# A two-layer decoder trunk on one core: compressed keys normed earlier, memory values split in halves, a lagging values product, gathers moved into the expert block

## The reference

```python
# layer 0 (even): sparse attention (8 heads, 2 kv groups) beside gated linear attention
q = rope(rmsnorm(q, q_g), positions)
kc = rope(rmsnorm(compress(k_cmp), k_g[0]), pos_blk_end)    # 31 compressed blocks
p_c = masked_softmax(einsum('bsghd,bcgd->bghsc', q, kc) * scale, mask_c)
o_c = einsum('bghsc,bcgd->bsghd', p_c, vc)
# selected-block branch o_s and sliding-window branch o_w, each softmax(q k) v
o = g0 * o_c + g1 * o_s + g2 * o_w
# every layer: cross-attention into mem (256 positions, 4 heads of 256)
kv = rmsnorm(mem, mem_g) @ wkv;  k = rmsnorm(kv[:, :, 0]);  v = kv[:, :, 1]
# every layer: 16 experts, top 2 of one group of 4
y = sum over e of gates[:, e] * ((silu(gu[:, :384]) * gu[:, 384:]) @ w_out[e]),  gu = t @ w_in[e]
```

## Time and profile before

| | before |
|---|---|
| median of 3 runs | 1619.91 us (1617.14 to 1620.81) |
| profiled execution | 1616.9 us, span 1614.8 |
| TensorE busy | 1451.3 us, 90% |
| VectorE busy | 977.9 us, 61% |
| ScalarE busy | 770.5 us, 48% |
| GpSimd busy | 142.8 us, 9% |
| mean granted TensorE clock | 0.951 |
| last projection ends | 160.4 us |
| compressed block, attention block | 168.5 to 192.9, to 310.9 us |
| expert blocks begin | 652.6 and 1357.7 us |

### The profile page before, as it was taken

One profiled execution on the slowest core, in us unless ns is written; L12 is line 12 of the kernel. 1 busy time (PEld: TensorE's weight loads), 2 busy tenths in 40 slices (PEclk: granted clock), 3 DMA queues, 4 the chain that ended last, 5 costly groups with the idle time before them and its releaser, 6 DMA issues. The chain is left out here.

```text
span 1614.8 us, 19652 instructions
## 1 busy us (share of the span) xinstructions
PE 1451.3 (90%) x7753; PEld 1221.7 (76%) x7753; DVE 977.9 (61%) x1297; ACT 770.5 (48%) x1124; POOL 142.8 (9%) x159
## 2 busy tenths in 40 slices
PE   6999698879899888799999599999999896999993
PEld 5788566667688666799997478887887585999982
DVE  4473657574646436699996522455244526999974
ACT  3412555374424424577774233432143524877761
POOL 1000011200000000222211000000000002222210
PEclk9999799879999999899999799999999997999997
DMA  6723121032252043799986532321522064899965
GB/s 195 138 57 107 36 72 53 1 105 95 74 213 79 27 151 144 258 381 374 376 340 238 189 105 81 102 79 53 186 67 77 1 243 185 338 368 387 373 257 207
DMA packets 111005, 274.96 MB, mean 170 GB/s; under 512 B 41777, under 2 KB 44226, under 8 KB 106306
## 3 DMA queue, kind: packets, MB, share of 16 engines
q1 hardware_dynamic: 95506, 203.96, 36.5%
q10 hardware_dynamic: 5904, 52.96, 8.3%
q0 software_dynamic: 9504, 16.80, 2.8%
HBM read 266.27 MB, written 25.17 MB: 180 GB/s over the span
## 5 line engine op out<-in xcount | busy, mean ns | idle before, releaser
L185 DVE TENSOR_TENSOR w_lo<-w_stage,w_hi 128x2048 fp32r<-128x2048 f32 (+2 forms) x32 | 67.2, 2104 | 187.3 <-ACT w_hi L175 177.4
L175 ACT ACTIVATE w_hi<-w_stage 128x2048 fp32r<-128x2048 f32 (+2 forms) x36 | 63.9, 1780 | 235.0 <-PE bank L240 154.9
L200 DVE TENSOR_TENSOR w_lo<-w_stage,w_hi 128x2048 fp32r<-128x2048 f32 x42 | 96.1, 2289 | 62.0 <-ACT w_hi L194 36.1
L194 ACT ACTIVATE w_hi<-w_stage 128x2048 fp32r<-128x2048 f32 x38 | 72.7, 1915 | 101.6 <-PE bank L240 65.3
L2871 PE MATMUL bank<-e_wi_lo,e_hx_hi 128*128 128x384 f32 x256 | 86.7, 339 | 0.0
L2870 PE MATMUL bank<-e_wi_lo,e_hx_hi 128*128 128x384 f32 x256 | 86.6, 338 | 0.0
L240 PE MATMUL bank<-w_hi,h_sg_hi 128*128 128x512 f32 x192 | 76.6, 399 | 4.1 <-DVE h_sg_lo L2293 2.1
L2726 DVE TENSOR_TENSOR e_wi_lo<-e_room,w_hi 128x1536 fp32r<-128x1536 f32 x40 | 68.6, 1752 | 11.6 <-ACT w_hi L2722 11.4
L240 PE MATMUL bank<-w_hi,h_sg_lo 128*128 128x512 f32 x192 | 75.3, 392 | 0.0
L240 PE MATMUL bank<-w_lo,h_sg_hi 128*128 128x512 f32 x192 | 75.3, 392 | 0.0
L2730 POOL DMA_INDIRECT e_tok<-moe_h,moe_slots x32 | 64.7, 2021 | 114.3 <-DVE moe_slots L2430 78.5
(11 more groups left out here) (529 smaller groups left out, 4194.2 us busy)
## 6 DMA issues: line engine op xcount, KB each, us to landing
e_room<-in_moe_w_in SPq DMA_DIRECT2D x88, 768.0 KB, 10.5
w_stage<-in_moe_w_in SPq DMA_DIRECT2D x40, 768.0 KB, 8.3
e_wo<-in_moe_w_out ACTq DMA_DIRECT2D x16, 1536.0 KB, 10.7
e_room<-in_moe_w_out ACTq DMA_DIRECT2D x14, 1536.0 KB, 11.1
w_stage<-in_x_wkv SPq DMA_DIRECT2D x16, 1024.0 KB, 5.3
w_stage<-in_sg_w_in SPq DMA_DIRECT2D x16, 1024.0 KB, 5.2
w_stage<-in_hyb_w_in SPq DMA_DIRECT2D x10, 1024.0 KB, 5.1
w_stage<-in_x_wq SPq DMA_DIRECT2D x8, 1024.0 KB, 5.1
```

Source lines behind the costliest of these rows:

```text
L175: act.activation(self.w_hi[h][:, :, :cols], self.stage[h][:, :, :cols], ACT.Copy)\
L185: dve.tensor_tensor(self.w_lo[h][:, :, :cols], self.stage[h][:, :, :cols], self.w_hi[h][:, :, :cols], ALU.subtract).then_inc(self.lo_done[ ...
L194: act.activation(self.w_hi[h][:, :, :cols], self.stage[h][:, :, :cols], ACT.Copy).then_inc(self.hi_done[h], 1)
L200: engine.tensor_tensor(self.w_lo[h][:, :, :cols], self.stage[h][:, :, :cols], self.w_hi[h][:, :, :cols], ALU.subtract).then_inc(self.lo_do ...
```

## The change

Four edits. First, in `hybrid_front` the root and the rest of the key norm move ahead of `group(LAST)`, and with them w_hi and w_lo of the first half of the memory value weights. Second, in `compressed_branch` TensorE makes the products of that half for both memory tiles (`values_half(pe, 0)`, 24 matmuls) after the scores; they go to banks 5 and 7, so scores use banks 2 and 3 and the transposes 6 and 4. VectorE adds the gates after the softmax's subtraction, and the w_lo half that stood ahead of the mask add is gone. Third, in `nsa_attention` the other half (`values_half(pe, 1)`) stands ahead of unit 0, units 1 and 2 lose their pieces, the eight pieces of group 3 move to units 3 to 6 and 8 to 11, its splits from units 3 and 4 to units 1 and 2, probT has two buffers, and TensorE issues the weighted product of unit u - 1 after the scores (and piece) of unit u. Fourth, the gathers of experts 0 and 1 and two w_lo quarters move from the end of `moe_front` to the start of `moe_experts`, in both layers.

```diff
@@ -612,9 +612,10 @@
                     act.activation(act1[:, kv, 0:N_CMP], m.psum[5 + kv][:, 0:N_CMP], ACT.Gelu_apprx_tanh).then_inc(gelued, 1)
                 act.wait_ge(out2, 2)
                 act.activation(vc[0:N_CMP], m.psum[7][0:N_CMP, P:2 * P], ACT.Copy).then_inc(v_here, 1)
-                group(LAST)
                 act.wait_ge(kc_mean, 1)
                 act.activation(kc_sq[0:N_CMP, 0, 0:KVH], kc_ss[0:N_CMP], ACT.Sqrt).then_inc(kc_root, 1)
+                m.half_hi(act, mkv.first, 0)
+                group(LAST)
...
@@ -714,12 +715,13 @@
                 link(dve.tensor_tensor(kc_sq[0:N_CMP], kc[0:N_CMP], kc[0:N_CMP], ALU.mult))
                 link(dve.tensor_reduce(kc_ss[0:N_CMP], kc_sq[0:N_CMP], AX.X, ALU.add))
                 dve.tensor_scalar(kc_ss[0:N_CMP], kc_ss[0:N_CMP], 1.0 / HD, EPS, ALU.mult, ALU.add).then_inc(kc_mean, 1)
-                group(LAST)
                 dve.wait_ge(kc_root, 1)
                 link(dve.reciprocal(kc_ss[0:N_CMP], kc_sq[0:N_CMP, 0, 0:KVH]))
                 link(dve.tensor_tensor(kc_n[0:N_CMP], kc[0:N_CMP], kc_ss[0:N_CMP].unsqueeze(2).to_broadcast([N_CMP, KVH, HD]), ALU.mult))
                 link(dve.tensor_tensor(kc_n[0:N_CMP], kc_n[0:N_CMP], kc_gain[0:N_CMP].unsqueeze(1).to_broadcast([N_CMP, KVH, HD]), ALU.mult))
                 rotate(dve, link, kc_r[0:N_CMP], kc_n[0:N_CMP], cos[0:N_CMP, T], sin[0:N_CMP, T], kc_tmp[0:N_CMP], KVH).then_inc(kc_done, 1)
+                m.half_lo(dve, mkv.first, 0)
+                group(LAST)
...
@@ -780,14 +782,15 @@
                     for h in range(HPG):
                         for g in range(KVH):
                             c0 = (i * HPG + h) * CP
-                            ins = pe.matmul(m.psum[4 + g][:, c0:c0 + CP], qkT[g * HD:(g + 1) * HD, h, i * P:(i + 1) * P],
+                            ins = pe.matmul(m.psum[2 + g][:, c0:c0 + CP], qkT[g * HD:(g + 1) * HD, h, i * P:(i + 1) * P],
                                             kcT[g * HD:(g + 1) * HD, :], start=True, stop=True)
                             if i == T - 1 and h == HPG - 1:
                                 ins.then_inc(scored[g], 1)
+                kv.values_half(pe, 0)
                 pe.wait_ge(normed, 1)
                 for g in range(KVH):
                     for i in range(T):
-                        ins = pe.transpose(m.psum[6 + g][:, i * P:(i + 1) * P],
+                        ins = pe.transpose(m.psum[6 - 2 * g][:, i * P:(i + 1) * P],
...
@@ -800,7 +803,7 @@
             @block.scalar
             def _(act):
                 kv.split_first_hi(act)
-                m.split_hi(act, kv.first)
+                m.half_hi(act, kv.first, 1)
...
-                dve.wait_ge(gb_in, 16)
-                dve.wait_ge(ga_t, 1)
-                dve.tensor_tensor(ga[:, :, :], m.psum[0][:, 0:T * 3 * HEADS].rearrange("p (t c) -> p t c", t=T), gate_b[:, :].unsqueeze(1).to_broadcast([P, T, 3 * HEADS]),
-                                  ALU.add).then_inc(g_lin, 1)
                 kv.split_first_lo(dve)
-                m.half_lo(dve, kv.first, 0)
...
@@ -831,6 +829,10 @@
                     ins = dve.tensor_tensor(cs[:, g], cs[:, g], cmax[:, g].unsqueeze(3).to_broadcast([P, T, HPG, CP]),
                                             ALU.subtract)
                 ins.then_inc(subbed, 1)
+                dve.wait_ge(gb_in, 16)
+                dve.wait_ge(ga_t, 1)
+                dve.tensor_tensor(ga[:, :, :], m.psum[0][:, 0:T * 3 * HEADS].rearrange("p (t c) -> p t c", t=T), gate_b[:, :].unsqueeze(1).to_broadcast([P, T, 3 * HEADS]),
+                                  ALU.add).then_inc(g_lin, 1)
...
@@ -884,14 +886,14 @@
 
         return m.psum[4][:, e * 256:(e + 1) * 256] if u < NARROW else m.psum[4 + e][:, :]
 
-    pieces = {1: (2, (4, 5)), 2: (2, (6, 7)), **{u: (3, (u - 6,)) for u in range(6, 10)}, **{u: (3, (u - 7,)) for u in range(11, 15)}}
+    pieces = {**{u: (3, (u - 3,)) for u in range(3, 7)}, **{u: (3, (u - 4,)) for u in range(8, 12)}}
 
     with ExitStack() as t:
         gate = m.sb(t, "gate", [P, T, HEADS, 3])
         compressed_branch(m, qkT, kcT, vbd, gaT, mix, gate, kv)
         m.phase()
         prob = m.sb(t, "prob", [P, 2, 2, S])
-        probT = m.sb(t, "probT", [P, 2, S])
+        probT = m.sb(t, "probT", [P, 2, 2, S])
...
+                def weighted(u):
+                    i, br, h = units[u]
+                    kt, n = keys(u), u // HPG
+                    if u % HPG == 0 and n >= 2:
+                        pe.wait_ge(scaled, n - 1)
+                    elif u == HPG:
+                        pe.wait_ge(kv.v_read, MT)
+                    for e in range(2):
+                        c0 = (e * HPG + h) * HD
+                        for j, k in enumerate(kt):
+                            ins = pe.matmul(m.psum[6 + n % 2][:, c0:c0 + HD], probT[:, u % 2, e, j * P:(j + 1) * P],
+                                            v_sw[:, k, br, e * HD:(e + 1) * HD], start=j == 0, stop=j == len(kt) - 1)
+                    if u % HPG == HPG - 1:
+                        ins.then_inc(summed, 1)
+
+                def kept(u):
+                    pe.wait_ge(kept_act, u + 1)
+                    if u >= NARROW:
+                        pe.wait_ge(kept_dve, u + 1 - NARROW)
+
                 score(0)
                 score(1)
-                for q in range(4):
-                    kv.values_piece(pe, 2, q)
-                for u, (i, br, h) in enumerate(units):
-                    kt = keys(u)
+                kv.values_half(pe, 1)
+                for u in range(NU):
                     if u == NARROW:
                         pe.wait_ge(kv.v_read, 2 * MT)
+                    if u:
+                        kept(u - 1)
                     for e in range(2):
                         pe.wait_ge(exped, 2 * u + e + 1)
-                        for j in range(len(kt)):
+                        for j in range(len(keys(u))):
                             ins = pe.transpose(turn_bank(u, e)[:, j * P:(j + 1) * P],
                                                prob[:, u % 2, e, j * P:(j + 1) * P], m.ident[:, :])
                         ins.then_inc(turned, 1)
@@ -937,20 +959,10 @@
                         score(u + 2)
                     for q in pieces[u][1] if u in pieces else ():
                         kv.values_piece(pe, pieces[u][0], q)
-                    n = u // HPG
-                    if u % HPG == 0 and n >= 2:
-                        pe.wait_ge(scaled, n - 1)
-                    for e in range(2):
-                        if e == 0 or u < NARROW:
-                            pe.wait_ge(kept_act, u + 1)
-                        else:
-                            pe.wait_ge(kept_dve, u + 1 - NARROW)
-                        c0 = (e * HPG + h) * HD
-                        for j, k in enumerate(kt):
-                            ins = pe.matmul(m.psum[6 + n % 2][:, c0:c0 + HD], probT[:, e, j * P:(j + 1) * P],
-                                            v_sw[:, k, br, e * HD:(e + 1) * HD], start=j == 0, stop=j == len(kt) - 1)
-                    if u % HPG == HPG - 1:
-                        ins.then_inc(summed, 1)
+                    if u:
+                        weighted(u - 1)
+                kept(NU - 1)
+                weighted(NU - 1)
...
                     if u == 0:
                         kv.keep_first_values(act, 2, 0)
-                    elif u == 3:
+                        kv.keep_first_values(act, 2, 1)
+                    elif u == 1:
                         m.half_hi(act, kv.group(0, 3), 0)
                         m.half_hi(act, kv.group(0, 3), 1)
-                        kv.keep_first_values(act, 2, 1)
-                    elif u == 10:
+                    elif u == 7:
                         kv.keep_first_values(act, 3, 0)
+                    elif u == 12:
+                        kv.keep_first_values(act, 3, 1)
                     elif u == 15:
-                        kv.keep_first_values(act, 3, 1)
                         m.half_hi(act, kv.group(0, 0), 0)
...
-                    if u == 3:
-                        m.half_lo(dve, kv.group(0, 3), 0)
-                    elif u == 4:
-                        m.half_lo(dve, kv.group(0, 3), 1)
+                    if u in (1, 2):
+                        m.half_lo(dve, kv.group(0, 3), u - 1)
...
+    def values_half(self, pe, h):
+
+        m, g = self.m, self.group(0, 2)
+        pe.wait_ge(m.lo_done[h], g + 1)
+        if h == 0:
+            pe.wait_ge(self.lo0, KD)
+        for b in range(MT):
+            for kk in range(KH):
+                k = KH * h + kk
+                for term, (x_part, w_part) in enumerate(((self.hi, m.w_hi[h]), (self.hi, m.w_lo[h]), (self.lo, m.w_hi[h]))):
+                    ins = pe.matmul(self.value_bank(2, b)[:, :], x_part[:, k, b * P:(b + 1) * P], w_part[:, kk, :],
+                                    start=h == 0 and kk == 0 and term == 0, stop=h == 1 and kk == KH - 1 and term == 2)
```

(30 more changed lines are left out.)

14 lines of the change are left out of this document (7 added, 7 removed).

## The result

The changed kernel takes 1596.07 us (median of 4 runs, 1594.96 to 1596.61). The kernel before took 1619.64 us beside it (4 runs, 1617.14 to 1620.81). The ratio is 0.9859 with a 95% interval of 0.9846 to 0.9871: 1.4% less time, some 23 us. A later set of runs of the same kernel gave 0.9871 [0.9857, 0.9886]. The profiled execution took 1595.87 us, its span was 1594.1 us. The forecast was 1604 with a range from 1597: the direction was right, the size was too small, and the result is just outside the low end.

A forecast was written before the change was run, and what follows sets the result against it. TensorE, busy 90% of the span, was taken as the bound, gains coming only from its idle or half-rate time. Terms 3.6 + 2.2 + 9.1 + 1.2 = 16.1 us off 1616.9 gave 1600.8, plus 3.0 for the median: 1604, range 1597 to 1612.

The forecast's parts named there:

- Part 1: Last projection before the compressed softmax: compressed keys normed ahead of its read-outs, 3.6 us gained, bounds 3.0 and 4.0.
- Part 2: Compressed softmax: mask add right after the scores, 24 value matmuls in PE's wait; 2.2 us gained, bounds 3.5 gained, 0.5 lost.
- Part 3: Attention: value matmuls gone, lagged weighted product, moved pieces and splits; -9.1 us in sum.
- (a): Attention: 24 value matmuls have left this phase, -5.6 us.
- (b): Attention's wide units: the lagged weighted product removes PE's 6.4 us of probT waits but 1.4; -5.0 us, bounds -7.0 and 0.
- (c): Attention's narrow units: earlier double w_hi stalls PE 5.5 us where one wait was 3.8; net +1.5 us, bounds -3 and +6.
- Part 4: Start of the experts, both layers: gathers moved out of the front block's end, -1.2 us for both, bounds -3.5 and +5.
- The loop sets the attention: Rival, attention: the softmax loop, not PE, sets the pace; attention gains about 2 us, time 1611; chance 15%.
- The gathers collide: Rival, expert start: both gathers land after 8.8 us instead of 5.9, PE starts 2.9 later per layer, 1610; chance 15%.
- The block's end was held by something else: Rival, front block's end: not held by the gathers, so each is added whole, 7 us late per layer, 1619; chance 3%.
- The clock stays low: Rival, compressed softmax and attention: clock stays at 0.50 until unit 8, costing 20 us, time 1624; chance 5%.
- Better than forecast: Case, attention: probT waits all gone and the narrow units' stall hidden, time 1598; chance 10%.

## Why the prediction was right in direction and too small

The forecast's sum of stages was 16.1 us; the spans differ by 20.7 and the medians by 23.6. Point by point:

**Part 1, -3.6: right.** 4.0 measured (0.1 of it from upstream). No table load behind the read-outs, the halves hidden, last copy and stage start where the text put them (164.85 forecast, 164.51 measured).

**Part 2, -2.2: the step that failed.** It was 5.8. The failing sentence is that "the add starts right after the scores: about 7.2 after block start". The 7.04 us of the scores were taken over from before as their price. They were the duration of this work at the low clock, and the clock had fallen right behind the 3.65 us wait that part 1, in the same forecast, takes away. At full clock the scores take 3.76 and the add starts 4.2 after the block does, 3.0 earlier than I had. The values half follows from that: I had ten of 24 matmuls at full clock and PE 1.4 late for the transposes. In the kernel after it ran at the low clock for 3.4 us only and PE was not late. Transposes came 4.3 sooner after the block's start than forecast, the tail took 0.7 more, hence the 3.6 that the term was short. Putting the wait back, alone, gave back 3.5 us in the stage that no one had edited (22.1 for 18.6), and over all profiles the fall comes 3 to 7 us earlier with the wait than without: that shows the link. How much of it a given execution gets isn't fixed: over the eight profiles with this same stage and no long wait it took 18.6 to 21.0 us, 19.5 in the mean, by when the clock fell (169.0 at the one end, 166.3 at the other). So of the 3.5 only 1.1 lie outside that spread, 5.8 is at the good end, and an average gain is about a microsecond less. That part of the 5.8 is luck.

**Part 3, -9.1: the total right (10.1), the addends not separable.** (a) -5.6 and (b) -5.0 were added as if each stood alone. The runs say that (b) alone gives 5.6 and (a) without (b), with the new places of (c), 0.3: without the lag PE is idle for longer. With the lag (a) is worth 4.7 (112.6 with the half back in the attention, 107.8 without). Both together give the sum. (b) came out as written (6.4 became 1.1, where I left 1.4). (c) was put at +1.5 by a stall of 5.5; the stall is 3.7 in all, no longer than the 3.8 before. Perhaps that is because the lag gives PE something to do there; no run tries it alone. Placing the halves early was not a cost that the runs show.

**Behind the attention, unpriced: 1.0.** The block after it starts with a low clock for 6.8 us where it was 10.2. The first fence is the kernel before, the second the kernel after.

```profile
309.40:319.60 10.20, 8.72 (x20) 6.47 (x21) 3.21 (x4) 2.34 (x2) 6.38 (x3) 0.50 0.00 0
```

```profile
291.00:298.70 7.70, 7.70 (x20) 5.67 (x21) 3.21 (x4) 2.29 (x2) 5.26 (x2) 0.56 0.00 0
```

What set its length wasn't tried.

**Part 4, -1.2: 0.2 measured, and 0 by the run that undid it.** The reason I gave for the gain held: the front block's end did wait for the gathers, and that wait is gone. But of the load beside the gather I said 0.9 ("the load should be over by 650") and it is 2.0 in layer 0. The rule of the Trainium skill that I quoted pointed there; I priced it too low, inside my bounds of 5.0 to 8.8.

**The offset, +3.0.** I added the distance of before's median of three to its profiled run. Later medians of before, of 11 runs each, were 1617.9 to 1618.9, so part of the 3.0 was that sample, and the profiled run of after lies at its median. That is up to 3.0 of the 7.9 us between forecast and result, the largest piece beside part 2.

**The rivals.** *The loop sets the attention*: no; PE's waits in the wide units are 1.1. *The gathers collide*: in kind yes, 6.9 for the 5.9 I had, not the 8.8 that it took. *The block's end was held by something else*: no. *The clock stays low*: in the compressed block the opposite, 0.50 only at 169.0 to 172.4. In the attention it was low from 192.9 to 203.2, 10.2 us where it had been 6.8 before, and back well before unit 8. The Trainium skill (TensorE: Matmul & The Clock Gate, HAM oscillation) describes a kernel that loses its clock anew in each pause between short bursts. The kernel before agrees only in part: its clock fell once, at 166.1, and stayed low for 23.9 us; the change shortened the pause ahead of that (3.65 to 0.49) and filled the one in it (7.60). *Better than forecast* had 10% and was the one that came, for another reason than its own. The range's low end was 1 us short: the best bound of part 2 was 3.5 where 5.8 came. It let the clock come back early under the new matmuls, but not stay high under the scores.

## What to carry to other kernels

A duration read in a stretch with the clock at 0.50 is no price for the same work once the stall ahead of that stretch is edited: work the stage out at both levels and follow the clock past the edit. Work taken off the busiest engine is worth its time only if that engine doesn't then wait for the next copy; a product that lags a unit and work that leaves the loop should be judged as a pair. Moving a transfer out of a block's end swapped one wait for another here, until the block that it moved into started no large load beside it (7.21 us for 9.18).

## What the runs showed of the hardware that was not expected

- The same instructions, 64 small score matmuls, took 3.76, 3.91, 4.25, 4.99, 6.12 or 7.04 us by when the granted clock fell, and the whole stage, in the changed code, 18.6 to 22.1 us. Ahead of the fall PE was busy for 0.27 of 3.40 us in one case and for 4.20 of 4.20 us, with 64x32 products, in another. The low clock then lasted 13.6 us with PE busy for 12.90 of them (transposes, scores, the first products of the values), and 10.2 us with PE busy throughout.
- In layer 0 a gather of 128 rows landed after 4.9 to 5.0 us without and 6.9 us beside a single 1536 KB load that was issued 1.15 us before it; in layer 1 after 4.1 and 5.7.
- A block doesn't end before its gathers land. In the kernel before the last one was issued at 647.03 and landed 5.2 us later; no engine had work after 648.1, and the next block began at 652.6.
